# Gated-delta layers: where the sample groups' outer products and outputs stand, and the order of the walk over four chunks

## The chip, the cores and the metric

The kernel is one program on one core of a Trainium2 chip. The metric is the device time of one execution in microseconds; lower is better. TensorE (PE) does matrix products out of SBUF into eight PSUM banks (`ps[0]` to `ps[7]`), VectorE (DVE), ScalarE (ACT) and GpSimd (POOL) work on tiles, and SyncE (SP) only starts transfers. Each engine runs its own instructions strictly in the order of the program and waits on semaphores.

## The reference, cut to what matters

A trunk of four layers works on a prompt of 256 tokens and on 8 samples of one token each. Layers 0 and 3 mix by the gated delta rule (8 heads, 128 keys and 128 values each), layer 1 is an mLSTM, layer 2 an RWKV-7, and each is followed by a feed-forward block. The gated delta rule runs over the prompt in four chunks of 64 tokens:

```
sol = triangular_solve(a_mat + eye, [v*beta, k*beta*exp(g)])   # per chunk and head
u, w = sol
for chunk in 0..3:
    v_new = u - w @ S
    o     = q_dec @ S + qk @ v_new
    S     = S * g_last + k_dec.T @ v_new
```

Each sample is one step of the same rule from a state of its own: `S_s = S_s * g + outer(k, v_new)`, `o = q @ S_s`. Outputs go through an RMS norm per head, are multiplied by `silu(z)` and projected by `w_out`. All states are outputs too: 8 heads x 8 samples of 128x128 for each of the two layers, 4 MB.

## The kernel before

Activations lie with 128 features on the partitions and T = 264 columns, 256 of the prompt and 8 of the samples. One gated-delta layer (`gdn(j)` in each engine's program) goes through these stages.

**Input projection** (`split_linear`), with weights through a ring of five slots (`RING`) that SP fills in the order of the list `units`.

**The inverses** (`invert64`): 64x64 unit triangular matrices, 16 on each half of the partitions, are inverted by doubling, `l` = 0 to 5. In a level PE does the products P for `h` = 0 and 1 (banks 0 and 1), ACT copies them out, PE does the products Q for `h` = 0 and 1 (banks 2 to 5), and DVE subtracts those from X and Z. The next P(h=0) needs only the subtraction of h=0, and P(h=1) that of h=1. `fill` holds other work by place: (l, 0) and (l, 1) stand behind P of h=0 and of h=1, (l, 2) and (l, 3) behind Q of h=0 and of h=1. Before, PE has the samples' products at (0, 0), the queries' spread at (0, 1), the turn of chunk l-1 into token-major form at (l, 1) for l = 1 to 4 (`token_major`: keys into bank 7, values into bank 6), and the samples' outputs at (5, 1). DVE takes the keys out of bank 7 at (l, 3) (`keys`). ACT (heads 4 to 7) and POOL (heads 0 to 3) meanwhile multiply the samples' states `st` by their decays.

**The solves**: `solve_values`, `solve_keys` and `state_update(0)`.

**The walk** over the chunks, c = 1 to 3, on PE: w @ S into bank 2; wait for DVE's v_new (`v_ok`); `state_update(c)` (banks 4 and 5); `outputs(c)`, in which for each of four head pairs the product of the queries with the state and that of the scores with v_new alternate (bank 6 or 7); `outer_products(c)`; `output_columns(c - 1)`, four transposes into bank 3. An outer product has 8 rows (one for each sample) and 512 columns. `outer_products(n)` makes two pairs of them, one after the other into the same banks 0 and 1, so the second pair waits until DVE has added the first to `st`. DVE adds POOL's scaled state and the product (`s_ok`), adds the outer products (`add_outer`), and gates the output columns (`gate_columns`). ACT copies the outputs from PSUM, squares the copy, and turns DVE's sums into factors (`output_norm`). POOL scales the state by the chunk's decay (`G_ok`), multiplies the outputs by their factors (`scaled`), and starts the stores of the samples' states, two heads in a chunk.

**The end**: 24 transposes of `tail`, `output_columns(3)`, and the projection by `w_out`. The feed-forward weights are then split into `w_mlp`, which lies where `st` lies, so ACT waits for the states' stores (`out_projection`).

Every order is written out by hand; no planner has a say.

## Time and profile before

| | |
|---|---|
| median of 3 runs | 1891.06 us (1884.0 to 1895.47) |
| profiled execution | 1888.66 us, span 1886.9 us |
| busy share of the span | PE 95%, DVE 53%, ACT 42%, POOL 14% |
| share of the chain that ended last | PE 89%, DVE 6%, ACT 2%, issue 2%, DMA 2% |
| mean granted TensorE clock | 0.947 of 2.4 GHz |
| layer 0, inverses from level 1 / solves / walk and end | 147 to 190.5 / 190.5 to 199.5 / 199.5 to 252.5 us |
| layer 3, the same | 1547 to 1590.4 / 1590.4 to 1599.4 / 1599.4 to 1654.9 us |

### The profile page before, as it was taken

Reading aid. Unit: us, or ns where it says so; the run is one execution under the profiler, and the core shown is the slowest. Engines: PE = TensorE matmul, PEld = TensorE weight load, DVE = VectorE, ACT = ScalarE, POOL = GpSimd, SP = SyncE. Lnnn points to the kernel's source line nnn. Section 1 sums busy time; section 2 is a strip of 40 time slices with the busy share of each in tenths; the row PEclk is TensorE's granted clock in tenths of the full one; section 3 lists DMA queues with packets and bytes.
Section 4 is the critical chain, followed back from the end, with each engine's and each line's share of the span. In section 5 each row is a group of like instructions: output and inputs, shape, how many; then the busy total and the mean of one; then the engine's idle time right before and its main releaser. Section 6 shows DMA issues by size and latency. Waiting matters only on the chain.

```text
span 1886.9 us, 39671 instructions
## 1 busy us (share of the span) xinstructions
PE 1786.4 (95%) x17442; PEld 1618.0 (86%) x17442; DVE 990.8 (53%) x1575; ACT 799.6 (42%) x1463; POOL 266.2 (14%) x319
## 2 busy tenths in 40 slices
PE   7999899999999699998999999999998999999997
PEld 6998579999888279998787789799997998589997
DVE  5853436753444747744363254467547834447643
ACT  4745236633431046533331222465436644146533
POOL 5005221001000310002003221010000033220001
PEclk9999789999998599999998999999999999599999
DMA  9540146555640245554332200165556520255550
GB/s 280 178 134 4 46 133 203 186 192 157 214 144 1 78 152 183 191 186 131 118 121 86 72 4 7 59 196 186 192 179 208 179 69 3 79 172 181 192 178 24
DMA packets 230207, 249.70 MB, mean 132 GB/s; under 512 B 15792, under 2 KB 221966, under 8 KB 229950
## 3 DMA queue, kind: packets, MB, share of 16 engines
q1 hardware_dynamic: 220096, 215.27, 36.0%
q0 software_dynamic: 9632, 31.81, 5.8%
q8 instruction: 138, 2.26, 0.5%
q14 instruction: 33, 0.27, 0.0%
q10 hardware_dynamic: 308, 0.10, 0.0%
HBM read 229.23 MB, written 18.32 MB: 131 GB/s over the span
## 4 chain that ended last, share of the span: by engine, by line
PE 89%; DVE 6%; ACT 2%; issue 2%; DMA 2%; SPq 0%; POOL 0%; DVEq 0%; POOLq 0%; ACTq 0%
PE ps L662 87%; PE ps L666 2%; DVE tri L2069 1%; DMA ring<-in_gdn_w_in_dram 1%; DVE acts L2069 1%; DVE hn L2077 1%; DVE acts L2077 1%; ACT acts L1584 1%; DVE acts L2458 0%; ACT L1587 0%; DVE st L2069 0%; DVE tri L2080 0%; DMA acts<-in_state_gdn_conv_dram 0%; ACT rows L1584 0%; ACT hn L1584 0%
## 5 line engine op out<-in xcount | busy, mean ns | idle before, releaser
L2069 DVE TENSOR_TENSOR w_mlp<-ring,w_mlp 128x1024 fp32r<-128x1024 f32 x256 | 311.5, 1224 | 157.1 <-ACT w_mlp L1584 150.9
L662 PE MATMUL ps<-hn_split,w_mlp 128*128 128x264 f32 x3072 | 374.1, 284 | 0.0
L662 PEld LDWEIGHTS ps<-hn_split,w_mlp 128*128 128x128 f32 x3072 | 372.3, 188 | 0.5
L1584 ACT ACTIVATE w_mlp<-ring 128x1024 fp32r<-128x1024 f32 x256 | 268.9, 1053 | 244.2 <-PE ps L662 217.3
L662 PE MATMUL ps<-h_split,w_mlp 128*128 128x264 f32 x3072 | 371.8, 283 | 0.0
L662 PEld LDWEIGHTS ps<-h_split,w_mlp 128*128 128x128 f32 x3072 | 371.5, 188 | 0.0
L662 PE MATMUL ps<-acts,ring 128*128 128x264 f32 (+2 forms) x960 | 224.4, 395 | 5.0 <-DVE acts L2077 3.0
L662 PEld LDWEIGHTS ps<-acts,ring 128*128 128x128 f32 (+2 forms) x960 | 181.5, 191 | 45.0 <-issue 5.0
L1584 ACT ACTIVATE tri<-ps 128x264 f32<-128x264 f32 (+6 forms) x184 | 81.5, 445 | 291.5 <-PE ps L662 215.2
L662 PE MATMUL ps<-gdn_hi,w_gdn 128*128 128x264 f32 x1024 | 191.1, 287 | 7.3 <-DVE mixer_lo L2069 5.9
L662 PE MATMUL ps<-tri 64*64 64x64 f32 (+1 forms) x3634 | 152.8, 228 | 18.8 <-issue 13.5
L662 PEld LDWEIGHTS ps<-gdn_hi,w_gdn 128*128 128x128 f32 x1024 | 160.8, 190 | 9.3 <-issue 9.2
L1584 ACT ACTIVATE acts<-ps 128x264 f32<-128x264 f32 (+4 forms) x138 | 62.1, 457 | 247.6 <-PE ps L662 237.7
L662 PEld LDWEIGHTS ps<-tri 64*64 64x64 f32 (+1 forms) x3634 | 122.6, 137 | 43.6 <-issue 32.8
L662 PE MATMUL ps<-mixer_lo,w_gdn 128*128 128x264 f32 x512 | 146.0, 285 | 0.0
L2069 DVE TENSOR_TENSOR tri<-tri 128x264 f32<-128x264 f32 (+3 forms) x137 | 65.0, 475 | 101.9 <-ACT h_split L1584 101.6
L2902 POOL TENSOR_TENSOR tri<-tri 128x264 f32<-128x264 f32 x20 | 16.5, 823 | 689.9 <-ACT tri L1584 687.6
L2069 DVE TENSOR_TENSOR tri<-tri,ps 128x512 f32<-128x512 f32 x84 | 54.2, 684 | 112.4 <-PE ps L662 112.4
L662 PEld LDWEIGHTS ps<-mixer_lo,w_gdn 128*128 128x128 f32 x512 | 97.6, 191 | 0.0
L2069 DVE TENSOR_TENSOR w_gdn<-ring,w_gdn 128x1024 fp32r<-128x1024 f32 x64 | 77.7, 1217 | 21.0 <-ACT w_gdn L1584 21.0
L662 PE MATMUL ps<-mlstm_hi,w_mlstm 128*128 128x264 f32 x384 | 74.1, 293 | 9.0 <-ACT rows L1584 4.7
L2077 DVE SCALAR_TENSOR_TENSOR acts<-ps,cw,acts 128x253 f32<-128x253 f32 x144 | 69.3, 481 | 11.4 <-ACT acts L1584 7.5
(343 smaller groups left out, 2075.2 us busy)
## 6 DMA issues: line engine op xcount, KB each, us to landing
ring<-in_ffn_w_dram SPq DMA_DIRECT2D x128, 1024.0 KB, 5.3
ring<-in_gdn_w_in_dram SPq DMA_DIRECT2D x32, 1024.0 KB, 5.9
ring<-in_ml_w_in_dram SPq DMA_DIRECT2D x12, 1024.0 KB, 5.4
ring<-in_rw_w_rkv_dram SPq DMA_DIRECT2D x12, 1024.0 KB, 5.1
st<-in_state_gdn_S_dram POOLq DMA_DIRECT2D x2, 4096.0 KB, 25.1
ring<-in_gdn_w_out_dram SPq DMA_DIRECT2D x8, 1024.0 KB, 5.1
out_gdn_S_s_dram<-st POOLq DMA_DIRECT2D x16, 512.0 KB, 4.5
st<-in_state_mlstm_C_dram POOLq DMA_DIRECT2D x1, 4096.0 KB, 18.4
```

Source lines behind the costliest of these rows:

```text
L662: return nc.tensor.matmul(out, lhsT, rhs, start=start, stop=stop)
L666: return nc.tensor.transpose(out, in_, ident[0:n, 0:n])
L1584: return nc.scalar.activation(out, in_, f, bias=bias, scale=scale)
L2069: return nc.vector.tensor_tensor(out, in0, in1, op)
L2077: return nc.vector.scalar_tensor_tensor(out=out, in0=in0, scalar=s, in1=in1, op0=op0, op1=op1)
L2902: last = gp_.tensor_tensor(sq[:, 0, :], sq[:, 0, :], sq[:, k, :], ALU.add)
```

## The change

1. The eight pairs of outer products go into the inverses, one pair at each of the places (3, 0), (3, 3), (4, 0), (4, 3), (5, 0), (5, 1), (5, 2) and (5, 3), into banks 6 and 7, the banks of `token_major`. The first waits for both masked values `MVS`, which DVE now makes behind the keys of levels 1 and 2. DVE adds each pair at the same place, in levels 3 and 4 behind the keys of the level.
2. The samples' outputs move from (5, 1) to (2, 0), their norm's sum to (2, 3), their gating to DVE behind (4, 3).
3. In the walk, the queries' products with the state stand together in front of the wait for `v_ok` (`query_state`), the scores' products together behind `state_update(c)` (`scores`), for c = 3 in front of it. `output_columns(c)` stands one or two places later; those of chunks 2 and 3 behind the transposes of `tail`.
4. ACT squares straight from PSUM and copies afterwards; `output_norm(c - 1)` stands behind `evacuate(c)`. The last chunk isn't copied: DVE multiplies it out of bank 7.
5. The states' stores go from POOL to SP, into the list of ring loads. The wait for the prompt's state store leaves the way to the feed-forward block, since `S6[4]` and `MVS` now lie in `hn`.

```diff
-        S6 = {1: tri[:, 0], 2: tri[:, 2], 3: tri[:, 3], 4: tri[:, 0]}
+        S6 = {1: tri[:, 0], 2: tri[:, 2], 3: tri[:, 3],
+              4: hn[:].rearrange("p k t -> p (k t)")[:, 0:D].rearrange("p (h v) -> p h v", h=GH)}
+        OUTER = ((0, 0, 0), (0, 0, 1), (1, 0, 0), (1, 0, 1), (0, 1, 0), (0, 1, 1), (1, 1, 0), (1, 1, 1))
+        OUTER_AT = ((3, 0), (3, 3), (4, 0), (4, 3), (5, 0), (5, 1), (5, 2), (5, 3))
+        TL_BANKS = (4, 5, 0, 1, 6, 2)
...
-        MVS = [A(5).rearrange("p a b -> p (a b)")[:, D:2 * D], tri[:, 1].rearrange("p a b -> p (a b)")]
+        MVS = [hn[:].rearrange("p k t -> p (k t)")[:, D * g:D * (g + 1)] for g in range(2)]
...
                     for q in range(NP):
                         sp.wait_ge(su_ev, 8 + q)
                         sp.dma_start(o["rS_s"][0, :, 2 * q:2 * q + 2].rearrange("s h v k -> (h v) s k"), rS[:, q]).then_inc(
-                            rss_out, 16)
+                            ss_out, 16)
+                for j, first in enumerate(gdn_out):
+                    if n == first + RING:
+                        for i in range(GH):
+                            h = (0, 1, 4, 5, 2, 3, 6, 7)[i]
+                            sp.wait_ge(op_ev, 48 * j + 4 * (i // 2) + 4)
+                            sp.dma_start(o["gdn_S_s"][j, :, h].rearrange("s k v -> k s v"),
+                                         st[:].rearrange("p (s h) d -> p h s d", h=GH)[:, h]).then_inc(ss_out, 16)
                 if n >= RING:
 
                     used, value = units[n - RING][1]
...
+                def sample_norm():
+                    pe.wait_ge(osq_ok, count.seen(osq_ok))
+                    b = 6
+                    pe.wait_ge(*last_read[b])
+                    mm(ps[b][:, 0:GH * NS], ones[:], E6[:, 0]).then_inc(on_mm, count.up(on_mm))
+                    last_read[b] = on_ev, count.expect(on_ev)
+
+                def outer_products(n):
+                    g, pi, half = OUTER[n]
+                    if n == 0:
+                        pe.wait_ge(mv_ok, count.seen(mv_ok, 2))
+                    for b in range(2):
+                        r = slice(32 * (2 * pi + b), 32 * (2 * pi + b) + NS)
+                        pe.wait_ge(*last_read[6 + b])
+                        mm(ps[6 + b][:], krow[r, g * P:(g + 1) * P], MVS[g][r, 512 * half:512 * (half + 1)]).then_inc(
+                            op_mm, count.up(op_mm))
+                        last_read[6 + b] = op_ev, count.expect(op_ev)
+
+                fills = {(0, 0): sample_products, (0, 1): spread_queries, (2, 0): sample_outputs, (2, 3): sample_norm}
+                for c in range(4):
+                    fills[c + 1, 1] = lambda c=c: token_major(c)
+                for n, at in enumerate(OUTER_AT):
+                    fills[at] = lambda n=n: outer_products(n)
+                invert64(fills, X6, M6, Z6, PX6)
...
-                def outputs(c):
+                def query_state(c):
                     b = 6 + c % 2
                     pe.wait_ge(*last_read[b])
                     tok = slice(c * HD, (c + 1) * HD)
                     for hh in range(4):
                         cut = slice(hh * P, (hh + 1) * P)
-                        if c:
-                            for g, r in enumerate(halves):
-                                mm(ps[b][r, cut], QS[:, 4 * g + hh, tok], S6[c][:, 4 * g + hh, :], True, False)
                         for g, r in enumerate(halves):
-                            last = mm(ps[b][r, cut], QK6[r, 4 * c + hh, :], VK[r, c, hh, :], c == 0, True)
+                            mm(ps[b][r, cut], QS[:, 4 * g + hh, tok], S6[c][:, 4 * g + hh, :], hh == 0, False)
+
+                def scores(c):
+                    b = 6 + c % 2
+                    if c == 0:
+                        pe.wait_ge(*last_read[b])
+                    for hh in range(4):
+                        cut = slice(hh * P, (hh + 1) * P)
+                        for g, r in enumerate(halves):
+                            last = mm(ps[b][r, cut], QK6[r, 4 * c + hh, :], VK[r, c, hh, :], c == 0, c == 0 or hh == 3)
                     last.then_inc(od_mm, count.up(od_mm))
-                    last_read[b] = oe_ev, count.expect(oe_ev)
+                    if c < 3:
+                        last_read[b] = oe_ev, count.expect(oe_ev)
 
...
-                    pe.wait_ge(oz_ok, count.seen(oz_ok))
+                    if c < 3:
+                        pe.wait_ge(oz_ok, count.seen(oz_ok))
+                    else:
+                        pe.wait_ge(ol_ok, count.seen(ol_ok))
                     b = 3
                     pe.wait_ge(*last_read[b])
                     for hh in range(4):
                         last = tp(ps[b][:, hh * P:(hh + 1) * P], orow(c)[:, hh * P:(hh + 1) * P])
                     last.then_inc(oc_mm, count.up(oc_mm))
                     last_read[b] = o_ok, count.expect(o_ok)
-
...
                 count.seen(u_ev, 3)
                 pe.wait_ge(wt_ev, count.seen(wt_ev, 4) - 2)
-                outputs(0)
-                outer_products(0)
+                scores(0)
                 for c in range(1, 4):
                     pe.wait_ge(s_ok, count.seen(s_ok))
                     if c == 3:
@@ -1031,26 +1064,29 @@
                     last.then_inc(ws_mm, count.up(ws_mm))
                     last_read[b] = v_ok, count.expect(v_ok)
                     if c == 1:
-                        pe.wait_ge(osq_ok, count.seen(osq_ok))
-                        b = 3
-                        pe.wait_ge(*last_read[b])
-                        mm(ps[b][:, 0:GH * NS], ones[:], E6[:, 0]).then_inc(on_mm, count.up(on_mm))
-                        last_read[b] = on_ev, count.expect(on_ev)
                         pe.wait_ge(qs_ok, count.seen(qs_ok, 4))
+                    query_state(c)
+                    if c == 3:
+                        output_columns(1)
                     pe.wait_ge(v_ok, count.seen(v_ok))
-                    state_update(c)
-                    outputs(c)
-                    outer_products(c)
-                    output_columns(c - 1)
+                    if c < 3:
+                        state_update(c)
+                        if c == 2:
+                            output_columns(0)
+                        scores(c)
+                    else:
+                        scores(c)
+                        state_update(c)
                 count.seen(s_ok)
 
                 for n in range(6):
-                    b = (4, 5, 0, 1, 6, 7)[n]
+                    b = TL_BANKS[n]
                     pe.wait_ge(*last_read[b])
                     for r in range(4):
                         last = tp(ps[b][0:3 + NS, r * P:(r + 1) * P], tail[:, 4 * n + r, :])
                     last.then_inc(tl_mm, count.up(tl_mm))
                     last_read[b] = tl_ev, count.expect(tl_ev)
+                output_columns(2)
                 output_columns(3)
                 pe.wait_ge(o_ok, count.seen(o_ok, 4))
...
+                    if l == 2:
+                        ac.wait_ge(ot_ev, count.seen(ot_ev))
+                        act(E6[:, 0].rearrange("p (h s) -> p h s", h=GH), A(4)[:, :, SEQ:T], ACT.Square).then_inc(osq_ok, count.up(osq_ok))
...
+                    if l == 2:
+                        ac.wait_ge(on_mm, count.seen(on_mm))
+                        rsqrt(E6[:, 1], E6[:, 1], ps[6][:, 0:GH * NS], c(EPS), 1.0 / P, on_ev, on_ok)
...
-                    ac.wait_ge(oe_ev, count.own(oe_ev))
-                    act(osq(c_), orow(c_), ACT.Square).then_inc(osqr_ok, count.up(osqr_ok))
+                    act(osq(c_), ps[6 + c_ % 2][:], ACT.Square).then_inc(osqr_ok, count.up(osqr_ok))
+                    if c_ < 3:
+                        act(orow(c_), ps[6 + c_ % 2][:], ACT.Copy).then_inc(oe_ev, count.up(oe_ev))
...
-                    output_norm(c_)
+                    output_norm(c_ - 1)
+                output_norm(3)
                 for n in range(6):
...
                     dv.wait_ge(h1h_ok, count.seen(h1h_ok))
...
+                    g, pi, half = OUTER[n]
+                    for b in range(2):
+                        h = 4 * g + 2 * pi + b
+                        if half == 0:
+                            sc = sts_ac if g else st_sc
+                            dv.wait_ge(sc, count.seen(sc))
+                        dv.wait_ge(op_mm, count.seen(op_mm))
+                        part = st[:].rearrange("p (s h) d -> p h s d", h=GH)[:, h, 4 * half:4 * half + 4, :]
+                        tt(part, part, mats(6 + b), ALU.add).then_inc(op_ev, count.up(op_ev))
+
+                def sample_outputs():
+                    dv.wait_ge(ot_mm, count.seen(ot_mm))
+                    for g in range(2):
+                        last = copy(A(4)[:, 4 * g:4 * g + 4, SEQ:T],
+                                    ps[6][:, g * P:(g + 1) * P].rearrange("p (h n) -> p h n", h=4)[:, :, NS:2 * NS])
+                    last.then_inc(ot_ev, count.up(ot_ev))
...
+                def sample_gates():
+                    dv.wait_ge(on_ok, count.seen(on_ok))
+                    o_ = A(4)[:, :, SEQ:T]
+                    step(stt(o_, o_, vec2[:, V_GN + j:V_GN + j + 1], ALU.mult, hs8(E6[:, 1]), ALU.mult))
+                    tt(o_, o_, A(3)[:, :, SEQ:T], ALU.mult)
+
+                def level_end(l):
+                    keys(l - 1)
+                    if l == 1:
+                        dv.wait_ge(smp_ev, count.seen(smp_ev))
+                        masked_values(0)
+                    elif l == 2:
+                        masked_values(1)
+                    elif l == 3:
+                        add_outer(1)
+                    else:
+                        add_outer(3)
+                        sample_gates()
+
+                fills = {(l, 3): lambda l=l: level_end(l) for l in range(1, 5)}
+                fills[2, 0] = sample_outputs
+                for n in (0, 2, 4, 5, 6, 7):
+                    fills[OUTER_AT[n]] = lambda n=n: add_outer(n)
+                invert64(fills, X6, M6, Z6)
...
 
-                dv.wait_ge(ot_mm, count.seen(ot_mm))
-                for g in range(2):
-                    last = copy(A(4)[:, 4 * g:4 * g + 4, SEQ:T], ps[6][:, g * P:(g + 1) * P].rearrange("p (h n) -> p h n", h=4)[:, :, NS:2 * NS])
-                last.then_inc(ot_ev, count.up(ot_ev))
-                dv.wait_ge(smp_ev, count.seen(smp_ev))
-                masked_values(0)
                 dv.wait_ge(sp_mm, count.seen(sp_mm))
                 copy(S6[1][:, 0:4, :], mats(4))
                 copy(S6[1][:, 4:8, :], mats(5)).then_inc(s_ok, count.up(s_ok))
-                add_outer(0)
                 for c_ in range(1, 4):
                     dv.wait_ge(ws_mm, count.seen(ws_mm))
                     if c_ == 1:
                         dv.wait_ge(u_ev, count.seen(u_ev, 4))
                     tt(VK[:, c_], VK[:, c_], mats(2), ALU.subtract).then_inc(v_ok, count.up(v_ok))
-                    if c_ == 1:
-                        masked_values(1)
-                    row_squares(c_ - 1)
+                    if c_ == 3:
+                        row_squares(2)
+                        gate_columns(0)
                     dv.wait_ge(sp_mm, count.seen(sp_mm))
                     dv.wait_ge(G_ok, count.seen(G_ok))
                     for g in range(2):
                         part = S6[c_ + 1][:, 4 * g:4 * g + 4, :]
                         last = tt(part, part, mats(4 + g), ALU.add)
                     last.then_inc(s_ok, count.up(s_ok))
-                    add_outer(c_)
-                    gate_columns(c_ - 1)
-                    if c_ == 1:
-                        dv.wait_ge(os_z, count.seen(os_z))
-                        dv.wait_ge(on_ok, count.seen(on_ok))
-                        stt(A(4)[:, :, SEQ:T], A(4)[:, :, SEQ:T], vec2[:, V_GN + j:V_GN + j + 1], ALU.mult, hs8(E6[:, 1]),
-                            ALU.mult)
+                    if c_ < 3:
+                        row_squares(c_ - 1)
                 row_squares(3)
+                gate_columns(1)
+                dv.wait_ge(orn_ok, count.seen(orn_ok, 4))
+                ot = orow(3).rearrange("p (h v) -> p h v", h=4)
+                tt(ot, mats(7), bc(orn(3), P, 2), ALU.mult).then_inc(ol_ok, count.up(ol_ok))
+                gate_columns(2)
                 gate_columns(3)
...
-                def stores(n):
-                    for h in (2 * n, 2 * n + 1):
-                        load(o["gdn_S_s"][j, :, h].rearrange("s k v -> k s v"), sth[:, h], sts_out)
-
                 for c in range(1, 4):
                     po.wait_ge(s_ok, count.seen(s_ok))
                     gp_.tensor_tensor(S6[c + 1], S6[c], bc(gl[:, GH * c:GH * (c + 1)], P, 2), ALU.mult).then_inc(
                         G_ok, count.up(G_ok))
                     scaled(c - 1)
-                    if c == 1:
-                        gp_.tensor_tensor(A(4)[:, :, SEQ:T], A(4)[:, :, SEQ:T], A(3)[:, :, SEQ:T], ALU.mult).then_inc(
-                            os_z, count.up(os_z))
-                    po.wait_ge(op_ev, count.seen(op_ev, 4))
-                    stores(c - 1)
+                count.seen(orn_ok)
+                count.seen(op_ev, 16)
                 po.wait_ge(s_ok, count.seen(s_ok))
                 load(o["gdn_S_p"][j, 0].rearrange("h k v -> k h v"), S6[4], sp_out)
-                scaled(3)
-                po.wait_ge(op_ev, count.seen(op_ev, 4))
-                stores(3)
                 po.wait_ge(tl_ev, count.seen(tl_ev, 6))
                 trow = rowbuf(5, 3 + NS, 3 * D)
                 load(o["conv_p"][j, 0], trow[0:3, :], tl_out)
```

## Rows read from the trace of the kernel before

**Rows 1.** Busy time of the engines, clock and DMA in the stages of both layers.

```profile
core 0: us, PE busy (x) PEld busy (x) DVE busy (x) ACT busy (x) POOL busy (x), PEclk, DMA share, GB/s
199.50:252.50 53.00, 46.86 (x271) 26.33 (x267) 23.50 (x39) 10.35 (x24) 16.44 (x17) 0.65 0.26 74
...
1599.40:1654.90 55.50, 49.40 (x268) 27.17 (x266) 23.51 (x39) 10.45 (x24) 16.57 (x17) 0.60 0.25 73
```

**Rows 2.** Timeline of level 2 of layer 0's inverses: start, duration, what.

```profile
159.48 1.29 DVE L2069 TENSOR_TENSOR tri<-tri,ps 128x512 f32<-128x512 f32 x2 [0.58 <-PE ps L662]
...
160.68 0.68 DVE L2069 TENSOR_TENSOR acts<-ps,cols 128x512 f32<-128x512 f32 x1
...
160.91 1.15 PE L662 MATMUL ps<-tri 64*64 64x64 f32 x32 [0.55 <-DVE tri L2069]
...
162.02 1.97 PE L662 MATMUL ps<-ident,acts 128*64 128x128 f32 x32
...
163.92 4.88 PE L662 MATMUL ps<-tri 64*64 64x64 f32 x160
```

**Rows 3.** Timeline from the last level to the start of the solves.

```profile
186.21 1.15 PE L662 MATMUL ps<-tri 64*64 64x64 f32 x32 [0.55 <-DVE tri L2069]
...
190.53 1.09 PE L662 MATMUL ps<-vk,tri 64*64 64x128 f32 x16 [0.79 <-DVE tri L2069]
190.59 1.22 DVE L2069 TENSOR_TENSOR acts<-mh,rows 128x1024 f32<-128x1024 f32 x1
```

**Rows 4.** Timeline of layer 0's walk, chunks 1 and 2, and the end.

```profile
199.55 1.13 PE L662 MATMUL ps<-acts,rows 8*128 8x512 f32 x4
...
201.52 2.67 PE L662 MATMUL ps<-acts,rows 8*128 8x512 f32 x4 [0.84 <-DVE st L2069]
...
220.49 1.98 PE L662 MATMUL ps<-tri,hn 128*64 128x128 f32 x16
...
223.12 0.68 DVE L2315 TENSOR_REDUCE rstd<-acts 128x4 f32<-128x512 f32 x1
...
223.25 1.16 PE L662 MATMUL ps<-vk,tri 64*128 64x128 f32 x16 [0.79 <-DVE vk L2069]
223.83 0.30 ACT L1584 ACTIVATE rstd<-rstd,cst 128x4 f32<-128x4 f32 x1 [8.53 <-DVE rstd L2315]
...
224.44 1.04 POOL L2869 TENSOR_TENSOR acts<-acts,rstd 128x512 f32<-128x512 f32 x1 [10.17 <-ACT rstd L1584]
...
225.08 0.44 PE L662 MATMUL ps<-tri,acts 128*64 128x128 f32 x4
...
227.26 1.91 POOL L2877 TENSOR_TENSOR tri<-tri,gl 128x1024 f32<-128x1024 f32 x1
...
227.40 0.60 ACT L1584 ACTIVATE acts<-ps 128x512 f32<-128x512 f32 x1 [3.04 <-PE ps L662]
...
246.86 4.20 PE L666 MATMUL ps<-ident,tail 128*11 128x128 f32 x24
...
251.53 0.87 DVE L2077 SCALAR_TENSOR_TENSOR acts<-ps,vec,acts 128x256 f32<-128x256 f32 x2 [2.96 <-PE ps L666]
```

**Rows 5.** The clock in the stretches of the walk, and in 3.4 us of layer 2.

```profile
1198.70:1202.10 3.40, 3.14 (x7) 2.38 (x8) 1.07 (x4) 1.33 (x4) 0.00 (x0) 0.51 0.00 0
...
202.00:222.40 20.40, 19.34 (x98) 10.52 (x96) 8.78 (x15) 2.30 (x6) 5.06 (x5) 0.50 0.18 52
...
229.30:239.50 10.20, 9.41 (x52) 5.90 (x52) 5.23 (x9) 0.50 (x2) 2.65 (x3) 0.50 0.16 47
```

**Rows 6.** Outer products of layer 1 alone, PE busy without a break.

```profile
632.00:655.00 23.00, 23.00 (x29) 8.21 (x28) 15.31 (x19) 0.00 (x0) 2.69 (x3) 0.50 0.30 105
```

**Rows 7.** Critical chain behind the walk of layer 0: start, duration.

```profile
252.46 214.80 PE ps L662 x1666
```

**Rows 8.** The page's DMA issues: engine, count, KB each, median us from issue to landing.

```profile
ring<-in_ffn_w_dram SPq DMA_DIRECT2D x128, 1024.0 KB, 5.3
...
out_gdn_S_s_dram<-st POOLq DMA_DIRECT2D x16, 512.0 KB, 4.5
```

More of the change, by code:

```diff
@@ L398, in hybrid_trunk @@
         oc_mm = shT_mm
-        os_z = negc_ok
+        ol_ok = cs1_ok
         osqr_ok = gexp_ok
@@ L627, in state_stores @@
         def state_stores(i):
-            return 16 * sum((GH, MH, 0)[n % 3] for n in range(i + 1))
+            return 16 * (0, GH, GH, GH + NP, 2 * GH + NP)[i + 1]
         def prompt_stores(i):
@@ L996, in output_columns @@
                     last_read[b] = o_ok, count.expect(o_ok)
[L998 to L1008 removed]
+                    if c == 3:
+                        last_read[7] = last_read[b]
                 solve_values(0)
```

67 lines of the change are left out of this document (19 added, 48 removed).

## The prediction

> **What bounds the kernel now.** I read the page first: TensorE is busy 95% of the span and holds 89% of the chain that ended last. So the questions are what the change does to TensorE's own queue and to its clock. The windows by stage come next: the walk with its end takes 53.0 us in layer 0 and 55.5 us in layer 3, with PE busy nearly throughout, but at a mean clock of 0.65 and 0.60 [rows 1]. The busy share hides two things there: products that run at 1.2 GHz, and modelled ends that cover short waits. The timeline shows what stands in the stage: pairs of outer products, of which the second waits 0.84 us for DVE [rows 4], and behind it everything of the next chunk. After the walk the chain is TensorE without a break for 214.8 us [rows 7], so what the stage gives up is given up by the whole kernel, and what is done to transfers behind it is not.
>
> **The walk, at 2.4 GHz.** A product of one kind for all heads (x16) takes 1.1 us with its modelled end, 1.04 from start to start [rows 3, 4]. I count from the end of chunk 0's scores, 199.55 in layer 0 [rows 4].
> Chunk 1: w @ S, queries, update, scores, 4 x 1.04 = 4.2. DVE's subtraction (0.7) lies under the queries' product, so `v_ok` costs nothing; without that cover it would be 0.8 with the signals, as the wait in front of the update shows now [rows 4]. The next w @ S waits for the state: update's end at 3.1, two additions as in the inverses 1.29 [rows 2], signals 0.2: 4.6.
> Chunk 2: to the update's end 7.7, columns of chunk 0 0.6, scores to 9.4. The state is late: POOL's scaling stands behind `scaled(0)`, and that now behind ACT's `evacuate(1)`. Scores' end 4.2, square and copy 1.2, two small ACT instructions 0.6, `scaled` 1.04, scaling 1.91: 9.05 [rows 4], then DVE 1.3: w @ S of chunk 3 starts at 10.5, a wait of 1.1 us.
> Chunk 3: w @ S and queries to 12.6. `output_columns(1)` waits for bank 3: subtraction 0.7, reduction 0.68, gating 0.87 [rows 4] give 13.95. Columns, scores and update to 16.65. The first bank of the tail waits for DVE's additions, 18.05. Tail 4.2, columns 0.6, gating 0.87, columns 0.6, gating 0.87 [rows 4], with signals 25.5.
> Before, the same way took 252.46 - 199.55 = 52.9 us [rows 4, 7] and 55.5 in layer 3 [rows 1]. The walk gives 27.4 + 30.0 = 57.4 us.
> At 1.2 GHz a product is 1.98 [rows 4]. The same sum with 1.95 for each product, 1.1 for columns and 4.4 for the tail is 36.3 us, 10.8 more in each layer. That is the bound on the other side.
>
> **The inverses, at 2.4 GHz.** These are bound by PE's order, with one gap of 0.55 us in a level in front of P(h=1) [rows 2]. T is the end of Q(h=1).
> Level 2: the samples' outputs (0.4 us) fit into the gap. The values of `token_major` wait until DVE has done keys (2 x 0.68), masked values (1.22 [rows 3]) and the copy: 163.6 instead of 163.0, +0.65.
> Level 3: outer product 0 waits for both masked values: subtractions 1.29, keys 1.28, masked values 1.22, in all T + 3.9. P(h=1) is behind it and starts at 5.0, now at 1.6 (P 1.04 and the gap): +3.4.
> Level 4: pair 1 stands behind Q of level 3, and its second half needs bank 7, which `keys` frees at T + 2.7. One outer product alone takes 0.8 (a record 0.79 us at 1.2 GHz [rows 6], two records, half at 2.4 GHz). P to 4.55, pair 2 1.1, P(h=1) at 5.65: +4.1.
> Level 5: the same wait to 3.5, then P, pair 4, P, pair 5, Q, pair 6, Q, pair 7: 2 x 1.04 + 2 x 0.95 + 4 x 1.1 = 8.4. The solves start at T + 11.9, now 190.53 - 186.21 + 1.6 = 5.9 [rows 3]: +6.0. `solve_keys` waits 0.2 more for bank 6.
> Sum +14.3 us in a layer, 8.8 of it the eight pairs, the rest waits, 28.7 in both. DVE's additions (1.28 a pair) lie under P, Q and `token_major`; the samples' norm on ACT lies in ACT's idle time in front of level 3. If the waits came out at nothing, the term would be 2 x 8.8 = 17.6.
> Without the clock: 57.4 - 28.7 = 28.7 us gained.
>
> **The clock.** It fell to 1.2 GHz at 202.0 [rows 5], and what PE had done before is one pair of outer products from 199.55, a wait, and the next pair from 201.52 [rows 4]. It stayed low for 20.4 us with PE busy 19.3 of them [rows 5]. In layer 1, 23 us of outer products without any pause ran at 1.2 GHz throughout [rows 6]. So products of 8 rows don't hold the clock up. The Trainium skill ("TensorE: Matmul & The Clock Gate", Part 1, The HAM clock gate) has the gate follow how busy the PE has been recently. By that rule the pairs would keep the clock as other products do; the row of layer 1 speaks against it, and by the rule the sum would stay at the gain without clock loss.
> In the new inverses there are three stretches of some 3.5 us with waits and outer products only, longer than the 2.5 us before the fall at 202.0. Low stretches in this trace last 3.4 us at the least, 10.2 and 20.4 where outer products recur [rows 5]. A product of 1.04 becomes 1.95, so a low microsecond costs about 0.45. Estimates: level 3, followed by unbroken work, 3.4 us low, 1.5; level 4, with pair 2 between its P, 8 us low, 3.5; level 5, where pairs recur to the end, four pairs by 1.0, P and Q by 3.1, and some 5 us of the solves by 2.3, 9.4. In all 14.4 in a layer if every stretch trips it, 28.8 in both; nothing if none does. I take three quarters, 22, since a stretch only a little longer than one that did it need not do it each time. The walk then runs at 2.4 GHz: its waits are 1.5 us at the most and no outer products are left.
>
> **Edits at nothing.** The eight stores of a layer leave POOL, where they stood in front of the scaling, for SP, where behind them stand only ring loads that wait for the output projection anyway; their 4 MB move under the solves instead of beside the ring loads [rows 8]. PE doesn't wait behind the walk [rows 7], so this neither gains nor loses; if the stores were late, ACT's first `w_mlp` would be, and 4 MB at the walk's own traffic could cost a few us. ACT's square from PSUM and the missing last copy are in the sum above.
>
> **Sum.** -57.4 + 28.7 + 22 = -7 us: 1888.7 becomes 1882 in terms of the profiled execution. The median of the runs is 2.4 us above it, so I forecast 1884.
>
> **Rivals.**
> *The clock stays up in the inverses.* For it: the pieces of wide work between the pairs are as long as the pairs. Against: the fall at 202.0. It gives -28.7, 1862.
> *The waits come out small as well*, because PE's gap and DVE's order hide them: -57.4 + 17.6 = -40, 1851. Against it: DVE's instructions are added straight from their rows.
> *The clock stays low in the walk (slower).* If the level 5 fall holds through the solves and each short wait of the walk keeps it there, both walks cost 36.3: -57.4 + 21.6 + 28.7 + 28.8 = +22, 1913. For it: 20.4 us low with PE busy in the walk now [rows 5]. Against: outer products were in that stretch. It turns slower as soon as the walks keep the low clock for more than a third of their length.
> *The walk doesn't shrink as said*, because the chain over ACT, DVE and POOL (10 us waits of POOL for ACT's factors today [rows 4]) is some 8 us longer in each layer: +9, 1900.
>
> **Chances.** Forecast 0.45, with its own range of 1877 to 1892; clock stays up 0.22; small waits too 0.08; low in the walk 0.15; walk doesn't shrink 0.10. Half a per cent, 9.5 us, is about what a measurement of this kernel can tell from no change. Faster by more: 0.22 + 0.08 and 0.12 of the forecast's own, 0.42. Within: 0.39, the forecast's other part and some of the last case. Slower: 0.19. The range 1857 to 1905 leaves out the smallest-wait case and most of the low-clock walk.
>
> **What would show it.** In level 3 PE waits for DVE's masked values 2.5 us, in front of levels 4 and 5 about 2 us for the keys. The solves start some 14 us later plus the clock's loss; windows over the last three levels show a clock well under 1.00. From chunk 0's scores to the output projection 25 to 27 us at 1.00, with waits of 1 to 1.5 us behind POOL's scaling, in front of columns 1 and in front of the tail. The prediction fails if the clock is 1.00 in level 5, or low in the walk, or if the walk takes over 30 us at 2.4 GHz.

## The result, and the profile after

The changed kernel takes 1905.3 us (median of 9 runs, 1897.66 to 1907.4), the kernel before 1891.06 us in its 9 runs beside it (1881.82 to 1895.47): a ratio of 1.0074, interval 1.0049 to 1.0099. It is slower, by 14 us; I had forecast 1884, in a range of 1857 to 1905. The profiled execution took 1905.89 us (span 1904.1) at a mean clock of 0.941. On the page PE is at 94%, DVE 52%, ACT 42%, POOL 13%, and PE holds 88% of the chain that ended last.

All times below go by three stages that can be cut at the same instructions in every kernel: the inverses from the queries' spread in level 0 to the first solve, the solves with chunk 0's scores up to the first w @ S, and the walk up to the output projection. The windows of the kernel before, layer 0 and then layer 3 (PE, PEld, DVE, ACT, POOL busy, then the granted clock and DMA):

```profile
147.92:190.53 42.61, 39.63 (x1046) 37.09 (x1043) 17.79 (x30) 22.20 (x62) 23.69 (x17) 1.00 0.01 3
190.53:204.11 13.58, 12.74 (x152) 9.16 (x152) 4.54 (x8) 5.44 (x11) 1.90 (x1) 0.92 0.01 1
204.11:252.46 48.35, 43.05 (x259) 25.21 (x258) 21.53 (x36) 9.12 (x22) 16.40 (x17) 0.63 0.28 81
...
1603.98:1654.94 50.96, 45.66 (x259) 25.89 (x258) 21.73 (x37) 9.22 (x22) 16.61 (x17) 0.59 0.27 79
```

The same windows of the changed kernel, and within the first of them layer 0's three low stretches, the third of which runs on into the solves, and the part of the last level behind its waiting pair:

```profile
150.92:222.41 71.49, 65.43 (x1081) 49.12 (x1077) 29.83 (x48) 23.02 (x65) 24.50 (x17) 0.78 0.16 46
222.41:235.70 13.29, 13.29 (x146) 11.95 (x145) 2.57 (x4) 4.13 (x8) 1.90 (x1) 0.65 0.29 81
235.70:259.12 23.42, 17.31 (x234) 14.51 (x233) 12.21 (x22) 8.50 (x21) 9.36 (x9) 1.00 0.09 26
...
1564.29:1635.61 71.32, 65.33 (x1080) 49.10 (x1077) 29.84 (x48) 23.01 (x65) 24.48 (x17) 0.78 0.16 46
1635.61:1648.87 13.26, 13.26 (x147) 11.95 (x145) 2.57 (x4) 4.13 (x8) 1.90 (x1) 0.66 0.27 80
1648.87:1672.28 23.41, 17.31 (x235) 14.51 (x233) 12.21 (x22) 8.49 (x21) 9.31 (x9) 1.00 0.10 27
...
177.00:180.40 3.40, 3.32 (x40) 3.13 (x38) 0.76 (x2) 0.60 (x1) 2.58 (x3) 0.50 0.00 0
187.20:197.50 10.30, 10.00 (x92) 6.76 (x94) 2.81 (x5) 1.19 (x2) 2.53 (x2) 0.50 0.36 103
204.40:231.70 27.30, 26.92 (x226) 18.04 (x226) 8.54 (x15) 3.47 (x6) 0.00 (x0) 0.50 0.41 116
206.78:222.41 15.63, 15.63 (x146) 9.14 (x145) 6.34 (x11) 1.19 (x2) 0.00 (x0) 0.50 0.47 135
```

The walk is what it was meant to be: 48.35 and 50.96 us became 23.42 and 23.41, at full clock. The inverses grew from 42.61 to 71.49 us, and more than half of that is not work: the clock fell from 1.00 to a mean of 0.78. It fell three times: in level 3, in level 4, and for 27.3 us from level 5 far into the solves, with PE busy for 26.92 of them. Three stages together: 104.5 to 108.2 us in layer 0, 107.2 to 108.0 in layer 3.

The timeline of layer 0 (compare [rows 2 to 4]) shows what stands in front of each fall:

```profile
173.77 1.43 DVE L2108 TENSOR_TENSOR hn<-mh,rows 128x1024 f32<-128x1024 f32 x1
175.25 1.13 PE L675 MATMUL ps<-hn,rows 8*128 8x512 f32 x4 [2.49 <-DVE hn L2108]
...
187.50 2.07 PE L675 MATMUL ps<-hn,rows 8*128 8x512 f32 x2 [1.53 <-DVE tri L2108]
189.50 1.97 PE L675 MATMUL ps<-tri 64*64 64x64 f32 x32
...
204.78 1.22 PE L675 MATMUL ps<-hn,rows 8*128 8x512 f32 x1 [1.53 <-DVE tri L2108]
...
220.40 2.08 PE L675 MATMUL ps<-hn,rows 8*128 8x512 f32 x4
222.41 1.97 PE L675 MATMUL ps<-vk,tri 64*64 64x128 f32 x16
...
240.15 1.09 PE L675 MATMUL ps<-tri,hn 128*64 128x128 f32 x16 [0.37 <-DVE tri L2108]
...
245.75 1.09 PE L675 MATMUL ps<-tri,hn 128*64 128x128 f32 x16 [0.94 <-DVE tri L2108]
...
249.10 0.63 PE L679 MATMUL ps<-ident,acts 128*128 128x128 f32 x4 [1.39 <-DVE acts L2116]
...
253.23 2.79 PE L679 MATMUL ps<-ident,tail 128*11 128x128 f32 x24 [1.39 <-DVE hn L2108]
```

The three waits are there, for the masked values in level 3 and for the keys of levels 3 and 4. Each fall begins in one of them or within 2 us behind it. A pair that takes 1.1 us at 2.4 GHz takes 2.1 behind the second and third of them; P takes 1.97 instead of 1.15 [rows 2]. Behind the walk the chain is again PE without a break, so nothing was lost to the ring loads [rows 7], and the stores land as they did, now from SP [rows 8]:

```profile
259.12 216.39 PE ps L675 x1666
```

```profile
out_gdn_S_s_dram<-st SPq DMA_DIRECT2D x16, 512.0 KB, 4.6
```

### The profile page after: what moved, and what is told of

Its sections match the earlier page's. It is cut to its first block, busy times and chain, and to the rows that moved or that the text cites. A ratio compares the mean times of both kernels' runs of the same rounds, so it can differ in the third digit from the quotient of the medians.

```text
span 1904.1 us, 39660 instructions
## 1 busy us (share of the span) xinstructions
PE 1793.4 (94%) x17442; PEld 1631.8 (86%) x17442; DVE 992.1 (52%) x1579; ACT 797.0 (42%) x1461; POOL 248.9 (13%) x299
## 3 DMA queue, kind: packets, MB, share of 16 engines
q0 software_dynamic: 7328, 23.42, 4.2%
## 4 chain that ended last, share of the span: by engine, by line
PE 88%; DVE 6%; ACT 2%; DMA 2%; issue 2%; POOL 0%; SPq 0%; DVEq 0%; POOLq 0%; ACTq 0%
PE ps L675 86%; DVE tri L2108 2%; DMA ring<-in_gdn_w_in_dram 1%; PE ps L679 1%; DVE acts L2108 1%; DVE hn L2116 1%; DVE acts L2116 1%; ACT acts L1620 1%; DVE hn L2108 1%; DVE acts L2518 0%; ACT L1623 0%; DVE tri L2119 0%; DMA acts<-in_state_gdn_conv_dram 0%; POOL tri L2933 0%; ACT rstd L1620 0%
## 5 line engine op out<-in xcount | busy, mean ns | idle before, releaser
L675 PEld LDWEIGHTS ps<-tri 64*64 64x64 f32 (+1 forms) x3634 | 133.6, 146 | 58.9 <-issue 45.1
L675 PE MATMUL ps<-tri 64*64 64x64 f32 (+1 forms) x3634 | 167.3, 239 | 14.9 <-issue 13.5
```

Of the source, the lines that this page charges most:

```text
L675: return nc.tensor.matmul(out, lhsT, rhs, start=start, stop=stop)
```

## The experiments

**Both kernels again.** No edit. The changed kernel, first for a whole set of runs and then for one profiled execution (a fourth profile of it stands at the end of this section):

> The changed kernel, unchanged, for a second profile. Its first profile shows the two gated-delta layers together 4.5 us slower than before, from the end of level 0 of the inverses to the output projection (+3.7 in layer 0, +0.8 in layer 3), and 12.8 us lost elsewhere: 3.1 at the start, 1.2 in a feed-forward block, 3.1 in layer 1, 4.7 in layer 2's inverses, less 1.2. Theory A (elsewhere it is the clock's luck of one execution): the same stages show other differences this time, and the total stays within 1898 to 1907. Theory B (the shift of the work in time costs the same clock falls in every execution): layer 2's inverses show the 10.2 us at 1.2 GHz again, and layer 1 the longer low stretch.

> The changed kernel, a third profile. The first two gave 216.2 and 215.0 us for the two gated-delta layers (before: 211.7 and 212.8) and 1305.2 and 1298.7 between them. Theory (all three stretches trip the clock in both layers in nearly every execution): the inverses 69 to 72 in both, the walk 23.4 in both, sum 214 to 217.

Measured: 1899.43 us against 1885.71 on that chip (1.0064, interval 1.0046 to 1.0083), and 1903.41 in the one execution. The kernel before, one profiled execution each:

> The kernel before, unchanged, for a second profile. In the one profile of it the two gated-delta layers take 104.5 and 107.2 us from the queries' spread to the output projection, and the stages between them 1295.3, where five other kernels of this study took 1297 to 1305 for the same instructions. Theory (one profile's luck, since low stretches come and go by some us in layers 1 and 2 in every kernel): the middle takes 1297 to 1305 here too, and the gated-delta layers less than 211.7 together, since the median is 1886 to 1891. Rival (the shift of the work costs the later stages something fixed): the middle takes 1295 again.

> The kernel before, a third profile. Two profiles gave 1295.3 and 1294.6 us between the two gated-delta layers, eight of other kernels with the same instructions there 1297 to 1305. If that is luck of where low stretches begin, this one is as likely as not at 1298 or above; if the change costs the later stages something fixed, it is at 1295 again.

> The kernel before, a fourth profile, with the same question: 1295 between the two gated-delta layers if the change costs the stages there something fixed, 1298 or above as likely as not if it is luck.

Measured: 1891.93, 1897.72 and 1888.14 us. Cut at the same instructions, the three stages of both layers together are 211.7, 212.8, 212.0 and 211.6 us in four profiles of the kernel before, and 216.2, 215.0, 217.7 and 215.3 in four of the changed one. In all eight changed layers the inverses take 69.8 to 72.6 us and the walk 23.4; each has the three waits and three falls, low for 37.5 to 44.4 us together with the solves, and every fall begins in a wait or within 2.6 us behind it. So inside the gated-delta layers the change costs 4.0 us in the mean, and the four profiles of one kernel lie clear of those of the other; the remainder of the 14 us lies elsewhere (last experiment).

**All but the move of the outer products.** Outer products, masked values and their additions stand in the walk, as before; all else is as in the changed kernel: the walk's new order, the samples' outputs in the inverses, ACT's part and the stores on SP.

```diff
                 fills = {(0, 0): sample_products, (0, 1): spread_queries, (2, 0): sample_outputs, (2, 3): sample_norm}
...
-                for n, at in enumerate(OUTER_AT):
-                    fills[at] = lambda n=n: outer_products(n)
...
                 scores(0)
+                outer_products(0)
+                outer_products(1)
...
+                    outer_products(2 * c)
+                    outer_products(2 * c + 1)
```

> The reordered walk with the eight pairs of outer products back in it, two pairs behind each chunk in banks 0 and 1 as before; the samples' outputs stay in the inverses. Theory (the walk's 29 us come from the outer products leaving it, for their own time, their waits and the clock that they let fall): the clock falls in the walk again, to a mean of 0.6 to 0.7, the walk takes 45 to 50 us where it took 52.9 before and 23.4 in the changed kernel, the inverses 44.5; kernel 1891 - 2 x 5 = 1881. Rival (the order of the walk alone gives most): the walk takes under 38 us and the kernel is at 1865 or under.

1871.88 us, 0.9918 (0.9889 to 0.9948): faster than both kernels. Layer 0:

```profile
148.14:190.22 42.08, 39.99 (x1049) 37.38 (x1045) 18.41 (x33) 22.93 (x65) 23.69 (x17) 1.00 0.01 3
190.22:203.81 13.59, 12.75 (x153) 9.16 (x154) 4.34 (x6) 5.16 (x10) 1.90 (x1) 0.93 0.00 1
203.81:242.14 38.33, 32.69 (x258) 22.34 (x257) 21.59 (x36) 7.87 (x19) 9.38 (x9) 0.80 0.46 128
```

The walk takes 38.3 us, less than the 45 to 50 I expected, because its clock rose as well, from 0.63 to 0.80. PE stands without a product for 5.3 us of the walk before and for 5.6 here, so what the order gives shows in the clock and not in shorter waits. These parts of the change are worth 10.5 and 13.1 us in the three stages (94.0 in both layers). So the rest of it, the outer products in the inverses, costs 14 us a layer: it takes 15 out of the walk and puts 29 into the inverses.

**The waits taken away.** DVE takes the keys, and makes the masked values, in front of the subtractions of Q instead of behind them.

```diff
+                def before_q(l):
                     keys(l - 1)
...
+                for l in range(1, 5):
+                    fills[l, 1] = lambda l=l: before_q(l)
```

> DVE takes the keys out of bank 7 and makes the masked values in front of Q's products of the same level, where it sits idle for 4 to 5 us, in place of behind them. Theory (DVE's place for the keys makes three waits of 2.5, 1.5 and 1.5 us, the waits and the outer products together let the clock fall, and the fall costs some 14 us a layer and 4 more in the solves): all three waits go, the clock stays at 1.00 through the inverses, the way from level 1 to the solves takes 43.7 + 8.8 = 52.5 us where the changed kernel takes 72.6, the solves 9.1 where it takes 13.3, and the kernel 1905 - 2 x 24 = 1857. Rival (the outer products alone let the clock fall, waits or not): the waits go, the clock still falls in level 5, 1905 - 2 x 10 = 1885. Rival (the waits aren't what orders the levels): 1900 to 1905.

1866.71 us, 0.9882 (0.9842 to 0.9921), runs from 1861 to 1872. Windows of layer 0, of layer 3 with its two low stretches, and of layer 0's level 5, and the start of that level:

```profile
149.33:200.05 50.72, 50.18 (x1080) 40.92 (x1077) 30.21 (x48) 22.93 (x65) 25.68 (x17) 1.00 0.20 57
200.05:209.51 9.46, 9.09 (x146) 8.10 (x145) 2.58 (x4) 4.08 (x8) 1.90 (x1) 1.00 0.53 154
...
1535.64:1591.33 55.69, 55.15 (x1080) 44.04 (x1077) 30.30 (x48) 22.93 (x65) 25.66 (x17) 0.89 0.21 59
1591.33:1604.36 13.03, 13.03 (x148) 11.72 (x146) 2.57 (x4) 4.13 (x8) 1.90 (x1) 0.67 0.29 82
...
1569.20:1572.70 3.50, 3.50 (x52) 3.38 (x50) 0.72 (x3) 0.60 (x1) 1.27 (x1) 0.51 0.92 269
1582.90:1600.00 17.10, 17.10 (x150) 12.46 (x150) 5.23 (x8) 2.28 (x4) 0.00 (x0) 0.50 0.54 153
...
190.57:200.05 9.48, 9.48 (x147) 5.88 (x145) 7.10 (x13) 1.20 (x2) 0.00 (x0) 1.00 0.64 183
```

```profile
189.51 1.13 PE L675 MATMUL ps<-hn,rows 8*128 8x512 f32 x4
190.57 1.15 PE L675 MATMUL ps<-tri 64*64 64x64 f32 x32
191.65 1.64 PE L675 MATMUL ps<-hn,rows 8*128 8x512 f32 x4
```

The three waits are gone (single pairs still take up to 1.6 us in place of 1.1), and where the clock stays up the inverses take 50.72 us, 8.1 more than before: PE is busy for 10.55 us more and without a product for 2.44 less, since the pairs stand in its old gaps. That is the price of the pairs where the clock doesn't fall. In layer 3 the clock fell nevertheless, for 3.4 us in level 4 and for 17.1 us from level 5 into the solves, with PE busy throughout. Low time in both layers is 20.5 us where the changed kernel has 82. So the waits are the main cause of the falls and not the only one. The profile is the fastest of four runs (1861.35 to 1872.34), so falls can be more in the others. I had expected 1857, with no fall.

**The waits filled.** Work is added, nothing taken away: 12, 8 and 8 products of 128 rows stand in the three waits. They go into bank 6 and are overwritten.

```diff
                     g, pi, half = OUTER[n]
+                    if n in (0, 1, 3):
+                        pe.wait_ge(*last_read[6])
+                        for _ in range(12 if n == 0 else 8):
+                            mm(ps[6][:, 0:P], ones[:], pair[:])
                     if n == 0:
                         pe.wait_ge(mv_ok, count.seen(mv_ok, 2))
```

> In front of the first, second and fourth pair of outer products PE does 12, 8 and 8 more products of 128 rows and 128 columns into bank 6, which the outer product then overwrites; the waits for DVE stay. This holds the clock and changes no wait. Theory (the fall is what the three stretches without wide products cause): the clock stays at 1.00 in the inverses, level 1 to the solves 43.7 + 14.3 = 58 us in place of 72.6, solves 9.1 in place of 13.3, kernel 1905 - 2 x 19 = 1867. Rival (the outer products in level 5 let it fall anyway): falls at the start of level 5 or in it, 1905 - 2 x 5 = 1895. Rival (the extra products only delay): 1905 or more.

1880.63 us, 0.9955 (0.9934 to 0.9976): PE has 28 more products in a layer, and the kernel is 19 us faster than the changed one beside it (1899.43). Windows of layer 0, and eight of the added products in the timeline:

```profile
148.87:211.39 62.52, 61.38 (x1137) 49.27 (x1133) 30.03 (x48) 23.05 (x65) 24.52 (x17) 0.93 0.18 53
211.39:224.51 13.12, 13.12 (x147) 11.81 (x145) 2.57 (x4) 4.13 (x8) 1.90 (x1) 0.66 0.28 81
```

```profile
181.86 2.05 PE L675 MATMUL ps<-pair,ones 128*128 128x128 f32 x16
```

At 2.05 us for eight, the 28 take some 7 us where the waits took 5.6. Levels 3 and 4 kept the clock; level 5 lost it all the same, late (low from 203.2 to 220.2), and the solves paid. I had expected 58 and 9.1 us here. A fall in an unbroken alternation of pairs and P or Q is left to explain.

**More rows.** The outer products take 32 rows instead of 8; the other rows are zeros, so the result is the same.

```diff
-                        r = slice(32 * (2 * pi + b), 32 * (2 * pi + b) + NS)
+                        r = slice(32 * (2 * pi + b), 32 * (2 * pi + b) + 32)
```

In the changed kernel:

> The changed kernel with outer products of 32 rows in place of 8: the further 24 rows are zero in the masked values, so nothing else changes, and PE's time for each is the same. Theory A (what the engine's rows do counts for the clock, so products of 8 rows hold it up hardly at all): with four times the rows some falls in level 5 or their length go, low time in inverses and solves drops from 41 us in layer 0 and 3 to 25 to 35, kernel 1888 to 1896. Theory B (the waits set the falls, the rows don't matter): low time 37 to 41 as in two profiles of the changed kernel, 1899 to 1905.

1884.56 us against 1889.39, 0.9985 (0.9953 to 1.0017), runs from 1874.76 to 1900.94: some 15 us faster than the changed kernel with 8 rows (1899.43 and 1.0064 on the same chip). Layer 0 is like the changed kernel's (clock 0.80 and 0.63), layer 3 is not: its falls in levels 3 and 4 are there, the third is not.

```profile
1552.82:1616.97 64.15, 58.17 (x1080) 45.60 (x1077) 30.07 (x49) 23.02 (x65) 24.47 (x17) 0.89 0.17 47
1616.97:1626.08 9.11, 9.09 (x147) 8.11 (x146) 2.25 (x4) 4.08 (x8) 1.90 (x1) 1.00 0.51 147
```

In the kernel before:

> The kernel before with outer products of 32 rows in place of 8, the further rows zero in the masked values. Theory (rows count for the clock): low time in the walk falls from 35 and 42 us to under 25, the walk from 48 and 51 to 40 to 45, kernel 1870 to 1882. Rival (the waits between the pairs set it): no change, 1886 to 1891.

1876.09 us against 1887.48, 0.996 (0.9928 to 0.9991). Walk of both layers, 48.35 and 50.96 us before:

```profile
203.79:243.36 39.57, 33.37 (x260) 19.44 (x259) 21.46 (x37) 9.06 (x22) 16.18 (x16) 0.87 0.33 95
...
1599.40:1642.92 43.52, 37.33 (x259) 21.27 (x258) 21.56 (x37) 9.06 (x22) 16.11 (x16) 0.76 0.30 87
```

The same instructions in the same order; rows of zeros alone give 8.8 and 7.4 us (in the seven profiles with 8 rows these walks take 47.7 to 51.1).

**No waits, pairs spread, with 8 and with 32 rows.** The keys early as above, and one pair fewer in level 5.

```diff
-        OUTER_AT = ((3, 0), (3, 3), (4, 0), (4, 3), (5, 0), (5, 1), (5, 2), (5, 3))
+        OUTER_AT = ((3, 0), (3, 2), (3, 3), (4, 0), (4, 3), (5, 0), (5, 2), (5, 3))
```

> The kernel with DVE's keys and masked values early, and the pairs of outer products at (3,0), (3,2), (3,3), (4,0), (4,3), (5,0), (5,2), (5,3): one pair fewer in level 5. With the pairs as they were, the clock held through layer 0's inverses and fell in layer 3's at level 5 (11.8 us there and 8.6 in the solves, 8.5 us longer). Theory (the density of outer products in level 5 is what is left to trip it): it holds in both layers, way from the queries' spread to the solves 50.7 in both, kernel 1858 to 1862. Rival (any pairs at all can trip it, by chance): one of the two layers still shows a low stretch, 1862 to 1872 as before the move.

> The same with outer products of 32 rows. If the rows count for the clock: no low stretch in inverses or solves in any execution, all runs within 1856 to 1862, no second group of slower runs. If they don't: as the kernel with 8 rows.

With 8 rows 1858.51 us, 0.9826 (0.9792 to 0.986), runs from 1849 to 1867; with 32 rows 1849.19 us, 0.9781 (0.9754 to 0.9808), runs from 1847 to 1851. Layer 3 with 8 rows, in the slowest of its six runs:

```profile
1536.34:1594.52 58.18, 57.64 (x1082) 45.83 (x1078) 30.38 (x48) 22.91 (x65) 25.66 (x17) 0.85 0.20 57
1594.52:1608.17 13.65, 13.65 (x148) 12.24 (x146) 2.57 (x4) 4.13 (x8) 1.90 (x1) 0.63 0.27 78
```

and with 32:

```profile
1530.58:1581.32 50.74, 50.20 (x1081) 40.88 (x1078) 30.46 (x49) 22.91 (x65) 25.66 (x17) 1.00 0.23 65
1581.32:1590.42 9.10, 9.09 (x146) 8.10 (x145) 2.25 (x4) 4.08 (x8) 1.90 (x1) 1.00 0.41 119
```

```profile
189.21 1.13 PE L675 MATMUL ps<-hn,rows 32*128 32x512 f32 x4
```

These two differ in rows alone. With 32 rows the clock stays at 1.00 in all three stages of both layers, which take 83.2 us each. A pair takes 1.13 us at this clock, as one with 8 rows does. It is the best version of the study, 40 us below the kernel before beside it (1889.39). The profile with 8 rows is one of 1867.23 us; its two fastest runs, 1849.39 and 1851.12, are as fast as those with 32 rows, at the same mean clock (0.965 and 0.966). So with 8 rows and no waits the clock falls in some executions and perhaps in none of the stages in others, against my expectation that it would hold; with 32 rows all six runs lie within 4 us.

**Where the rest is.** Outside the gated-delta layers PE has the same instructions in both kernels. The suspicion was that a mere shift of the schedule against the clock's falls costs there. The kernel before, with 8, 16 or 24 products that are overwritten, in level 4 of layer 0 alone:

```diff
                         pe.wait_ge(*last_read[b])
+                        if j == 0 and c == 3 and b == 7:
+                            for _ in range(8):
+                                mm(ps[7][:, 0:P], ones[:], ident[:])
```

> The kernel before, with 8 extra products of 128 rows and 128 columns (overwritten afterwards) in front of the token-major products of level 4 of layer 0 alone: everything behind them stands some 2 us later, and nothing else differs. Theory: the stretches outside the gated-delta layers cost more merely because the schedule stands elsewhere against the clock's falls; then the way from layer 0's output projection to layer 3's inverses, 1295 us in three of four profiles of the kernel before, is 1297 to 1305 here, as in the changed kernels, and the three shifts differ among themselves. Rival: only the change does that; then it stays at 1295, and the total is that of before plus 2 us.

> As the one with 8, with 16 extra products, some 4 us later. Theory: 1297 to 1305 us between the layers. Rival: 1295, and the total is that of before plus 4 us.

> As the one with 8, with 24 extra products, some 6 us later. Theory: 1297 to 1305 us between the layers. Rival: 1295, and the total is that of before plus 6 us.

> The changed kernel once more: another profile of it. 1304 us; between the layers 1298 to 1305 us if its extra over before there is alignment alone, and 71.5, 13.3 and 23.4 us for inverses, solves and walk as in the other profiles.

Medians 1890.37, 1891.43 and 1893.72 against 1889.46 (0.9998, 1.0014 and 1.0016, every interval with 1 in it), the changed kernel 1904.58 (1.0074, 1.0049 to 1.0098). The products added put the rest of the program 2, 3.8 and 5.6 us later; the medians rise by 0.9, 2.0 and 4.3, which is within the noise. From layer 0's output projection to layer 3's inverses the profiles take:

| kernel | us in each profile |
|---|---|
| before | 1295.3, 1294.6, 1301.8, 1295.2 |
| before, shifted by 2, 3.8 and 5.6 us | 1298.8, 1294.6, 1294.6 |
| before, with 32 rows | 1300.8 |
| changed | 1305.2, 1298.7, 1297.7, 1301.6 |
| the six other versions of the changed kernel | 1297.2 to 1302.7 |

A shift can move this part (the first one), and mostly does not. The changed kernel is 4.4 us above the first seven in the mean (1300.8 to 1296.4), though the ranges overlap, and the kernel before with 32 rows has its 1300.8 too. Two places make most of it. One is the first 3.4 us of the output projection, the kernel before and then the changed one:

```profile
252.46:255.86 3.40, 3.40 (x15) 2.94 (x16) 0.00 (x0) 0.00 (x0) 1.38 (x3) 1.00 0.96 251
```

```profile
259.12:262.52 3.40, 3.40 (x8) 2.69 (x9) 0.00 (x0) 0.00 (x0) 0.00 (x0) 0.53 0.31 84
```

The tail of the new walk is transposes between waits of 1.0 to 1.4 us, and the clock falls right behind it. That costs 1.7 us in three of four profiles, in none of the seven without the change; behind layer 3's walk it is the same, 1.7 us in three of four. That the tail is the cause is not shown: the kernels with early keys, with filled waits and with spread pairs of 32 rows have the same walk and tail, and no fall behind them. The other is a piece of layer 1 (the kernel before, the changed one, and the one shifted by 2 us):

```profile
564.71:604.68 39.97, 36.37 (x201) 31.53 (x200) 20.32 (x54) 9.72 (x29) 0.00 (x0) 0.87 0.00 0
```

```profile
573.49:616.23 42.74, 39.14 (x202) 34.29 (x200) 20.33 (x54) 9.72 (x29) 0.00 (x0) 0.81 0.00 0
```

```profile
567.30:610.11 42.81, 39.21 (x201) 34.37 (x200) 20.32 (x54) 9.73 (x29) 0.00 (x0) 0.81 0.00 1
```

By its clock the same work takes 39.9 to 40.1 us or 41.6 to 42.8; the longer occurs in one of the seven and in all four changed profiles. What picks it is open: one shift does it, so does the kernel before with 32 rows (41.6 us), other shifts do not. In the mean of four profiles each, the layers make 4.0 us, the part between them 4.0, the end 1.5 and the start 0.3, and that is all of the 9.8 us by which the profiled spans differ (1899.7 to 1889.9). The medians differ by 14: single executions of one kernel lie up to 17 us apart, and four are too few to meet the median.

## Why the prediction was wrong

The total is 21 us above the forecast of 1884, on the other side of no change.

**The walk (right).** 25.5 us forecast from chunk 0's scores to the projection, 23.4 measured, at 1.00. The waits were 0.37, 0.94, 1.39 and 1.39, in the places named. It gives 29.5 and 32.1, 61.6 us, against 57.4. Most of the 2.1 us is one row: the 4.2 us of the tail [rows 4] were taken partly at 1.2 GHz (the kernel before was low there, 0.51 from 242.9 to 249.8), and at 1.00 the tail takes 2.6. (The terms of the chain to POOL's scaling, 9.05, add up to 8.95, which changes nothing.)

**Pairs and waits in the inverses (right).** 14.3 us a layer forecast, 8.8 of them pairs. The pairs are 8.1 net of the gaps that they fill (the experiment without waits), the waits 2.49, 1.53 and 1.53, 5.6 in sum against 5.5.

**The clock in the inverses (the step that failed).** "In all 14.4 in a layer if every stretch trips it, 28.8 in both; nothing if none does. I take three quarters, 22." Both halves of it were short. Every stretch trips it, in all eight layers of four profiles. And one layer loses more: 71.49 less 42.61, 8.1 and 5.6 is 15.2 us in the inverses, and the solves with chunk 0's scores take 13.29 against 9.02 before (190.53 to 199.55 [rows 3, 4]), 4.3. That is 19.5 in layer 0 and 19.3 in layer 3, 38.8 in both, 17 above the term. Taking three quarters is 7 of these 17: no stretch was spared. The other 10 are the sizes, and the mis-sized part is mainly level 5: I let the fall end some 5 us into the solves, and it lasted to 231.7, 9.3 us in. Spread over the busy time of the three low stretches, the 19.5 us come to an estimate of 1.6, 4.9 and 13.0, where the forecast had 1.5, 3.5 and 9.4. The trace of the kernel before had a warning that I did not use: where outer products recur, layer 3's walk was low for 37.5 us, not only for the 10 and 20 that I named.

```profile
1601.50:1639.00 37.50, 34.46 (x174) 18.80 (x174) 15.38 (x26) 4.03 (x10) 9.70 (x9) 0.50 0.19 57
```

**The sum.** -61.6 + 27.4 + 38.8 = +4.6, against -7 forecast; the three stages of this pair of profiles differ by 3.7 and 0.8, 4.5. With every stretch tripping, the forecast's own terms gave 0. Then come some 6 us outside the layers, in the mean of the profiles, that no step had; the projection's start (1.7 us twice, in three of four) is a part of them. That the sum misses these stages by only 12 us is in part luck: the walk gave 4 us more than said, which hid as much of the clock's loss.

**The edits at nothing (right).** The stores landed in 4.6 us, and PE did not wait behind the walk.

**The rivals.** That the clock stays up is what the kernel with early keys does in layer 0 of its profile, not this one. That it stays low in the walk did not occur: 1.00 in both. The slower side was reached by more clock loss in the inverses, a case that had no chance of its own. The range's upper end should have carried "all stretches trip, and level 5 runs through the solves".

**On the cause of a fall.** The prediction said that products of 8 rows don't hold the clock up, with layer 1's row against the rule of the Trainium skill ("TensorE: Matmul & The Clock Gate", Part 1, The HAM clock gate) that the gate follows how busy the PE has been. The experiments bear out the direction: with PE busy 57.64 of 58.18 us the clock still fell with 8 rows (0.85) and, with PE busy 50.20 of 50.74, not with 32 (1.00); by PE's busy share alone the two would be alike. They amend the weight: with 8 rows and no waits layer 0's inverses stay at 1.00 (in the one profile of each such kernel; in the spread one the clock fell in the solves instead), and filling the waits takes away two of the three falls. Waits and narrow products each do their part, and with neither, no fall is left in the one profile, and all six runs lie within 4 us. 32 rows with the waits left in still fall in levels 3 and 4. Why a given execution falls and another does not stays open, as with the spread pairs of 8 rows.

## What to carry to other kernels

Work moved off a loop keeps its own time and brings its waits along; when it is narrow, what it does to TensorE's clock in its new place can cost more than the work. Move first what releases it on the other engines (here the keys and masked values, 33 us: 1899.43 to 1866.71), then the work. And don't price a clock fall by the length of the stretch that trips it: the last one here went on through 9.3 us of the solves, in which PE had no break.

## What the hardware showed that I had not expected

The clock falls and rises by more than PE's being busy. Pairs of 8-row products alternating with P and Q without a pause ran 15.63 us at 0.50 in the changed kernel (206.78 to 222.41) and 9.48 us at 1.00 with early keys (190.57 to 200.05): in these two stretches the same mix kept the level that it found. It doesn't always: in layer 3 with early keys the clock fell in the middle of it. Rows of zeros made a difference too: 32 rows instead of 8 cost no time (1.13 us a pair either way) and gave 9 us in the spread version, 11 in the kernel before (2 to 14 by the interval) and some 15 in the changed one.
